# The order of VectorE's and ScalarE's work around the gated product, in the attention of two hybrid layers

## The reference, cut to what matters

```python
h = rmsnorm(x, norm_g)
a_b, a_c, a_x, a_z, c_q, ..., c_z, gate_pre = split(h @ w_in)
u = a_c * a_x
conv = conv_b                                   # causal, 3 taps along the tokens
for tap in range(3):
    conv = conv + up[:, tap:tap + S] * conv_w[tap]
y_a = a_b * conv * silu(a_z)
y_b = attention(q, k, v) * silu(b_z)            # 8 heads, causal ("mla")
y_c = dilated_attention(dq, dk, dv) * silu(c_z) # 8 heads, 3 groups ("dil")
g_a, g_b, g_c = split(sigmoid(gate_pre + b_gate))
merged = g_a * (y_a @ w_out_a) + g_b * (y_b @ w_out_b) + g_c * (y_c @ w_out_c)
x = x + merged @ w_o
```

## Time and profile before

| | |
|---|---|
| median of 3 runs | 1950.78 us |
| span of the profiled execution | 1955.9 us |
| PE busy | 1865.2 us, 95% |
| DVE busy | 753.2 us, 39% |
| ACT busy | 586.3 us, 30% |
| POOL busy | 533.0 us, 27% |
| chain that ended last | PE 63%, DMA 28%, DVE 6%, ACT 1% |

### The profile page before, as it was taken

The page is one execution under the profiler, slowest core; times in us unless marked ns, Lnnn a source line. Parts: engine busy times, 40 slices in busy tenths (PEclk is TensorE's granted clock), DMA queues, the critical chain, the costliest instruction groups (busy, mean ns, idle before and its releaser), DMA issues.

```text
span 1955.9 us, 26950 instructions
## 1 busy us (share of the span) xinstructions
PE 1865.2 (95%) x10980; PEld 1197.3 (61%) x10980; DVE 753.2 (39%) x1365; ACT 586.3 (30%) x1054; POOL 533.0 (27%) x224
## 2 busy tenths in 40 slices
PE   7999999989999899999999999999999999999997
PEld 6778889977789799856584444434434443343443
DVE  4776563446864543675533212112112211111112
ACT  4544455435554455444421011101101110110111
POOL 5767656767766567301000000000000000000000
PEclk9999999999999999999979999999999999999999
DMA  8554423555554334522679999999999999999995
GB/s 309 194 194 171 153 100 117 199 178 202 206 182 146 114 130 147 217 78 87 237 288 385 428 429 428 429 429 429 429 429 410 428 428 429 429 428 428 429 428 226
DMA packets 111989, 563.39 MB, mean 288 GB/s; under 512 B 4864, under 2 KB 24448, under 8 KB 87200
## 3 DMA queue, kind: packets, MB, share of 16 engines
q1 hardware_dynamic: 111904, 562.17, 71.6%
HBM read 561.11 MB, written 1.05 MB: 287 GB/s over the span
## 4 chain that ended last, share of the span: by engine, by line
PE 63%; DMA 28%; DVE 6%; ACT 1%; issue 1%; SPq 0%; DVEq 0%; ACTq 0%
DMA ring<-in_e_in_dram 27%; PE bank L1900 15%; PE score L1063 12%; PE bank L1890 10%; PE mixed L1100 4%; PE bank L1867 4%; PE bank L853 2%; PE bank L863 2%; PE mixed L1984 1%; PE bank L894 1%; PE flip L1967 1%; DVE ring L2491 1%; PE score L1083 1%; PE bank L1123 1%; PE score L1953 1%
## 5 line engine op out<-in xcount | busy, mean ns | idle before, releaser
L2278 POOL TENSOR_TENSOR w_lo<-ring,w_hi 128x1024 fp32r<-128x1024 f32 (+1 forms) x216 | 523.2, 2432 | 277.6 <-ACT w_hi L2177 276.8
L1063 PE MATMUL score<-ring,space 128*64 128x512 f32 x2000 | 448.8, 594 | 36.6 <-DMA ring<-in_e_in_dram 35.5
L1063 PEld LDWEIGHTS score<-ring,space 128*64 128x64 f32 x2000 | 140.7, 137 | 333.6 <-issue 248.1
L2177 ACT ACTIVATE w_hi<-ring 128x1024 fp32r<-128x1024 f32 (+1 forms) x216 | 226.2, 1049 | 228.6 <-PE bank L1900 120.8
L1900 PE MATMUL bank<-h_hi,w_hi 128*128 128x256 f32 x896 | 261.8, 292 | 0.0
L1900 PE MATMUL bank<-h_lo,w_hi 128*128 128x256 f32 x896 | 253.2, 283 | 0.0
L1900 PE MATMUL bank<-h_hi,w_lo 128*128 128x256 f32 x896 | 252.2, 281 | 0.0
L1339 ACT ACTIVATE space<-space 128x512 f32<-128x512 f32 x32 | 20.2, 631 | 693.5 <-DVE space L1673 693.5
L1100 PE MATMUL mixed<-ring,space 128*64 128x512 f32 x1024 | 226.8, 595 | 0.3 <-ACT space L1343 0.3
L1673 DVE TENSOR_SCALAR space<-score 128x512 f32<-128x512 f32 x32 | 22.2, 693 | 405.9 <-PE score L1063 405.9
L1900 PEld LDWEIGHTS bank<-h_hi,w_hi 128*128 128x128 f32 x896 | 169.9, 190 | 4.6 <-issue 4.4
(11 more groups left out here) (365 smaller groups left out, 2383.3 us busy)
## 6 DMA issues: line engine op xcount, KB each, us to landing
ring<-in_e_in_dram SPq DMA_DIRECT2D x125, 2048.0 KB, 25.1
ring<-in_e_out_dram SPq DMA_DIRECT2D x64, 2048.0 KB, 22.0
ring<-in_w_in_dram SPq DMA_DIRECT2D x42, 2048.0 KB, 7.6
ring<-in_w_ada_dram SPq DMA_DIRECT2D x16, 1024.0 KB, 5.3
ring<-in_w_o_dram SPq DMA_DIRECT2D x6, 2048.0 KB, 8.3
ring<-in_w_qkv_dram SPq DMA_DIRECT2D x4, 2048.0 KB, 9.8
ring<-in_w_ada_dram SPq DMA_DIRECT2D x4, 2048.0 KB, 9.5
ring<-in_w_out_a_dram SPq DMA_DIRECT2D x2, 2048.0 KB, 8.5
```

Of the source, the lines that this page charges most:

```text
L1063: ins = pe.matmul(score[HALF * blk:HALF * blk + HALF, which * W:(which + 1) * W], xs[:, 2 * j + r, HALF * hh:HALF * hh + HALF], wk[:, blk ...
L2177: act.activation(split_part(w_hi, k), raw_part(k), ACT.Copy).then_inc(hi_done, 1)
L2278: pool.tensor_tensor(split_part(w_lo, k), raw_part(k), split_part(w_hi, k), ALU.subtract).then_inc(lo_done, 1)
```

## The change

Three moves, no instruction added or removed. DVE: `low_branch` and `convolve` stand ahead of `gated(j-1)` instead of behind it. ACT: the second "az" unit's tanh moves from the end of step 6 to step 7, behind `unflip_probs(6, 0)`. ACT: `round_branch` moves from the end of steps 6 and 9 into steps 7 and 10, behind the first `split_to`.

```diff
@@ ScalarE @@
+            def late(u):
+                return UNITS[u][0] == "az" and UNITS[u][2][-1] == 1
...
                     if j > 0:
                         unflip_probs(l, j - 1, 0)
+                    for u in DONE_IN[j - 1] if j else ():
+                        if late(u):
+                            evacuate(l, u)
                     if j < NJ and len(STEPS[j]) == 1:
                         exp(l, j)
                     for r in range(len(ROUNDS[j - 1]) if j else 0):
...
                         if r == 1 and j < NJ and len(STEPS[j]) == 2:
                             exp(l, j)
                         split_to(l, NQ_PREP + sum(QUARTERS[:j]) + r + 1 + PARTS)
+                        if r == 0 and j in (7, 10):
+                            round_branch(l, 1 if j == 7 else 0)
                     for u in DONE_IN[j]:
-                        evacuate(l, u)
+                        if j == NJ or not late(u):
+                            evacuate(l, u)
                     split_to(l, NQ_PREP + sum(QUARTERS[:j + 1]) + PARTS)
-                    if j in (6, 9):
-                        round_branch(l, 1 if j == 6 else 0)
@@ VectorE @@
                     if j < NJ:
                         divide(l, j)
+                    if j in (7, 10):
+                        low_branch(l, 0 if j == 7 else 1, 1 if j == 7 else 0)
+                    if j in (3, 4):
+                        convolve(l, j - 3)
                     if j > 0:
                         gated(l, j - 1)
...
-                    if j in (7, 10):
-                        low_branch(l, 0 if j == 7 else 1, 1 if j == 7 else 0)
-                    if j in (3, 4):
-                        convolve(l, j - 3)
```

## The result

The changed kernel takes 1957.45 us (median of 8 runs, 1952.35 to 1962.1), the kernel before 1951.1 us (8 runs, 1949.05 to 1954.76). The ratio is 1.0029, with a 95% interval of 1.0018 to 1.0040: 5.7 us slower (3.5 to 7.8). That is just beyond the 0.2% that the forecast of 1952.7 took as its bound for "the same": of its three outcomes the likeliest (0.60) did not come, and "slower" (0.25) did. The time lies within the range given, 0.5 us from its upper end.

What follows compares the result with a forecast made beforehand. PE bounds the kernel, busy 139.66 of 145.00 us in layer 0's attention. Idle +1.8 us, clock 4.8 coming against 4.7 going: +1.9 us on the 1955.9 span, less 5.1 for the runs' median, 1952.7 us; range 1945.5 to 1958.

Steps and rivals of the forecast that it cites:

- The convolution of step 3: DVE in attention: convolution meets three POOL operations, delays the gated product; new PE stall 3.7 us, bounds 0 and 3.7.
- Step 4: Second half of the convolution: gated product ends at about 246.6, PE waits 0.15 us; old 1.74 us stall goes.
- The flip copy ahead of the tanh: ACT, step 7: flip copy no longer waits; 2.15 us of stall and 1.6 us of clock go in each layer.
- the ledger: The prediction's count of gains and losses; old stalls of 5.33 us a layer and 4.7 us of clock go.
- The low branch of step 7: DVE: POOL holds its subtraction to 3.2 to 3.3 us, delaying the gated product; new PE stall 2.4 us.
- Step 10: Low branch ahead of the gated product at 324.86: hidden in DVE's idle time with 3 us to spare, cost 0.
- The clock: PE's low clock behind stalls: 4.7 us go, 1.6 us come behind three of four new stalls, 4.8 us.
- its own sign: The forecast is wrong if the clock is at 0.50 for more than 15 us of the two attentions.
- the first rival: The clock falls further behind the new stalls, 9.6 us instead of 4.8, so 1957.5 us; chance 0.22.
- The sum: PE idle +0.9 us a layer, +1.8 for two; with the clock +1.9 us in all, so 1952.7 us.
- The rivals with a free port: No POOL hold-up in steps 3 and 4, near 1938 us, 0.07; or in step 7's low branch, 1946.5 us, 0.10.
- the one with the clock up: Rival: the new stalls leave PE's clock up, -2.9 us, so 1947.9 us; chance 0.06.

Runs made afterwards that it cites:

- experiment 1: The kernel before with only the convolution of steps 3 and 4 moved ahead of the gated product: 1956.77 us, ratio 1.0027 to the kernel before.
- experiment 4: The changed kernel without the convolution's third tap, so two operations less in each convolution (result not the reference's): 1949.15 us, ratio 0.9987 to the kernel before.
- Experiment 8: The changed kernel with PE working a quarter ahead of its waits in values(3) and values(7): 1957.19 us, ratio 1.0014 to the kernel before.
- experiment 2: The changed kernel with DVE's order of before, so ACT's moves alone: 1946.91 us, ratio 0.9974 to the kernel before.
- experiment 3: The changed kernel with only the convolution back behind the gated product: 1953.4 us, ratio 1.0008 to the kernel before.
- experiment 7: The changed kernel with the low branch of step 7 moved between mask(7, 1) and divide(7): 1951.57 us, ratio 0.9989 to the kernel before.

## Why the prediction was right in mechanism and short in size

The mechanism of the two big new stalls came as it was laid down. The step that failed is a term of the sum, the clock, which was put at 4.8 us and measured 7.9; the forecast that the time would stay the same failed with it.

- *The convolution of step 3* (forecast: held by three POOL operations, gated product to 234.65, stall 3.7 us). Measured: 3.56 us. All six operations fell as laid down. Experiments 1 and 4 show it as the cause.
- *Step 4* (0.15 us, 0 to 0.5). Measured: 0, but not for the reason given. The forecast let POOL hold this half of the convolution, which was to take from 239.4 to 246.2. It met no POOL operation and took 2.9 us, so the gated product of job 3 waited 2.94 us for PE, not the other way round. That the price was right all the same is luck. Experiment 8 shows how narrow it was: with POOL earlier the stall is 4.3 us. The bounds had been too tight.
- *The flip copy ahead of the tanh.* Its gain of 2.15 us and the clock behind it came; by itself 5.1 us by the ratio of experiment 2, for both layers, where the ledger has 7.5. Of the rest, 0.7 us are the two new stalls of 0.36. The low clock that can follow the remaining stall of 1.74 us varies from one place to the next and may be more of it; that isn't shown.
- *The low branch of step 7* (2.4 us, bounds 0.4 and 2.5). Measured: 2.91 us, beyond the upper bound. The subtraction took 3.37, not 3.2 to 3.3, and DVE's small operation before the exp 0.87 us beside POOL instead of 0.16, a loss of 0.7 us where the forecast had allowed 0.15. Experiments 3 and 7 show it as the cause.
- *Step 10* (0). Measured: 0. The low branch takes 2.57 us at 324.29, and 3.27 us of idle time are left behind it, where 3 were forecast.
- *The clock* is the term that was mis-sized. The forecast took 1.6 us behind three of four stalls, 4.8 us. Measured in the trace, against flips of 0.59 us and quarters of 2.83 to 2.86 in the chain at full clock: flips and quarter are longer by 0.50 + 2.19 us behind the first stall, 0.50 + 2.09 behind the second, 0.50 + 2.15 behind the third and by less than 0.1 behind the fourth, 7.9 us in all. The falls before were 1.6, 1.6 and 1.5. So the number was right, three in four, but each fall cost 2.6 to 2.7 us and not 1.6: the flips and nearly the whole quarter ran at 0.50. The forecast had named its own sign for this, a clock at 0.50 for more than 15 us of the two attentions, and it was 20.5. This was the first rival (9.6 us, 1957.5), which was given 0.22, and in the main it is the one that came.
- *What stays open in it.* The length of the stall alone doesn't set the price of the fall. In the traces of experiments 1, 3 and 7 the same stalls of 3.56 and 2.92 us were followed by falls that cost 1.5 to 1.6 us, the size that was forecast. Each of these traces is of the fastest execution of its kernel, while the trace of the changed kernel is of a middling one (1957.81 us, the median is 1957.45). So the price of a fall behind the same stall varies from one trace to the next. Whether it varies between executions of one kernel too, and what decides it, no run shows.
- *The sum.* Idle: 6.47 us for 5.33 in each layer, +2.3 where +1.8 was forecast. Clock: 7.9 - 4.7 = +3.2 where +0.1 was forecast. Together +5.5 us, against 5.3 between the marks of the trace and 5.7 in the runs. Layer by layer this gives +4.8 and +0.7, where the marks show 4.7 and 0.6. It was the range, and in it the room left for this rival, that held the result, not the sum.

The rivals with a free port (0.07 and 0.10) fall by the DVE rows of the changed kernel, and by experiments 1, 3, 4 and 7; the one with the clock up (0.06) by the windows. The new stalls were to show as released by the gated product; the profile names no releaser, and the reading rests on the gated product's end, 0.1 us before each.

## What to carry to other kernels

Before moving work ahead of a short operation that frees a buffer, ask which in-order queue stands behind that buffer, and whether the work fits the idle time as it will really run there, beside its neighbour on the port; here 2.9 us of work took 9 us in one slot and 2.9 in the next. Cut such work into pieces that end when the waiting engine arrives, and put it where the neighbour rests: with ScalarE's moves kept, the same operations in four slots and the low branch behind the gated product turned 5.7 us of loss into 14 of gain. Price a stall of TensorE together with the clock behind it, which here was from nothing to nine tenths of the stall again, and differed by 1.1 us from one trace to another behind the same stall.

## What the runs showed of the hardware

- A DVE operation with two SBUF inputs, or a TENSOR_SCALAR from SBUF to SBUF, that starts while POOL's subtraction runs is held to that subtraction's end, however small it is: 0.48 us became 2.5, and an operation on two columns 0.87 for 0.16. In the ten traces of this case 923 such operations start inside one of POOL's subtractions, and none ends before it does. In the other order POOL is held: one operation of 2.40 us took 2.74 in the changed kernel, at 280.11, where a DVE operation with two SBUF inputs ran until 280.58. The Trainium skill, "SBUF — State Buffer", section "Who interferes with whom", has the rule (the port pair that the two share is locked for a whole instruction, and whoever starts second waits), and all traces here agree.
- Where POOL's subtractions stand back to back, each DVE operation beside them was held for one of them: in step 4 before, three operations took 1.48 and 5.01 us beside three subtractions of 7.3 us, and 5.02 and 2.31 in experiment 8. So what counts is how many of POOL's operations a sequence meets: the convolution's six took 2.9 us beside none and 8.9 to 9.0 beside three, and the four of experiment 4 took 5.9 beside two, which is how two operations less could save 3.1 us.
- The same stall in the same program is followed by the low clock in one place and not in the other (1.09 and 0.63 us for the same flips behind 2.91 and 2.92 us). Behind a stall of 1.74 us in the kernel before it was one place in two as well. Small differences between kernels of this kind need many executions, or marks in the trace on either side of the change.
